# Feed-forward down projections by seven products of half blocks

## What is computed

```python
def rmsnorm(x, g):
    xf = x.astype(jnp.float32)
    xf = xf * lax.rsqrt(jnp.mean(xf * xf, axis=-1, keepdims=True) + EPS)
    return (xf * g.astype(jnp.float32)).astype(x.dtype)

def swiglu_ffn(x, w_up, w_down):
    gate, up = jnp.split(x @ w_up, 2, axis=-1)
    return (jax.nn.silu(gate) * up) @ w_down

# in both layers
h = h + swiglu_ffn(rmsnorm(h, norm_ffn[l]), ffn_w_up[l], ffn_w_down[l])
```

## Time and profile before

| what | before |
|---|---|
| median of 3 runs | 1588.88 us (1588.54 to 1588.92) |
| span of the profiled execution | 1588.5 us |
| instructions | 26988 |
| TensorE busy | 1557.8 us, 98% |
| VectorE busy | 1050.6 us, 66% |
| ScalarE busy | 816.2 us, 51% |
| GpSimd busy | 812.8 us, 51% |

### The profile page before, as it was taken

How to read it: one execution, slowest core, us unless ns; L and a number is a source line. 1 busy time by engine, 2 the same in 40 slices (tenths; PEclk the granted TensorE clock), 3 DMA queues, 4 the chain that set the end, 5 groups by cost and what they waited for, 6 DMA issues and landing times.

```text
span 1588.5 us, 26988 instructions
## 1 busy us (share of the span) xinstructions
PE 1557.8 (98%) x10227; PEld 1356.5 (85%) x10227; DVE 1050.6 (66%) x1622; ACT 816.2 (51%) x1334; POOL 812.8 (51%) x459
## 2 busy tenths in 40 slices
PE   6999999999999999999999999999999999999997
PEld 4888888888887878478998998988788998998996
DVE  6887587597597859977734643664666762572555
ACT  4555455355356535376633542654666652453453
POOL 1444345345345439827655654654116665564653
PEclk8999999999999999999999999999999999999999
DMA  9322322322323365712332332352112333233231
GB/s 376 140 93 80 120 83 91 119 82 90 119 81 102 128 116 153 187 53 81 107 119 80 106 119 81 105 182 96 54 41 68 106 112 100 93 106 115 85 117 69
DMA packets 53640, 172.86 MB, mean 109 GB/s; under 512 B 5403, under 2 KB 11580, under 8 KB 53052
## 3 DMA queue, kind: packets, MB, share of 16 engines
q1 hardware_dynamic: 47296, 159.90, 30.6%
q10 hardware_dynamic: 6268, 11.95, 3.2%
HBM read 165.48 MB, written 6.36 MB: 108 GB/s over the span
## 4 chain that ended last, share of the span: by engine, by line
PE 79%; DVE 3%; issue 2%; ACT 2%; POOL 2%; DVEq 0%; ACTq 0%; POOLq 0%
PE gps L2026 13%; PE gps L2028 12%; PE gps L2027 12%; PE gps L2449 6%; PE gps L2451 6%; PE gps L2450 6%; PE aps L2449 3%; PE aps L2451 3%; PE aps L2450 3%; PE gps L2386 2%; PE gps L2084 1%; PE gps L2086 1%; PE gps L2085 1%; POOL w_lo L619 1%; PE aps L2527 1%
## 5 line engine op out<-in xcount | busy, mean ns | idle before, releaser
L619 POOL TENSOR_TENSOR w_lo<-w_raw,w_hi 128x1024 fp32r<-128x1024 f32 x172 | 437.4, 2547 | 545.9 <-ACT w_hi L741 545.8
L2026 PE MATMUL gps<-xa_hi,w_hi 128*128 128x512 f32 x767 | 306.6, 400 | 2.6 <-DVE xa_lo L1380 2.6
L2027 PE MATMUL gps<-xa_lo,w_hi 128*128 128x512 f32 x767 | 299.9, 391 | 0.0
L2028 PE MATMUL gps<-xa_hi,w_lo 128*128 128x512 f32 x767 | 299.8, 391 | 0.0
L741 ACT CAST w_hi<-w_raw 128x1024 fp32r<-128x1024 f32 x172 | 180.0, 1046 | 155.6 <-PE gps L2028 75.2
L2026 PEld LDWEIGHTS gps<-xa_hi,w_hi 128*128 128x128 f32 x767 | 144.6, 188 | 35.3 <-DVE xa_lo L1380 4.1
L2028 PEld LDWEIGHTS gps<-xa_hi,w_lo 128*128 128x128 f32 x767 | 144.6, 188 | 31.1
L2027 PEld LDWEIGHTS gps<-xa_lo,w_hi 128*128 128x128 f32 x767 | 144.8, 189 | 27.6
L2026 PE MATMUL gps<-xb_hi,w_hi 128*128 128x512 f32 x378 | 148.2, 392 | 0.0
L2028 PE MATMUL gps<-xb_hi,w_lo 128*128 128x512 f32 x378 | 147.2, 389 | 0.0
L2027 PE MATMUL gps<-xb_lo,w_hi 128*128 128x512 f32 x378 | 147.1, 389 | 0.0
(11 more groups left out here) (428 smaller groups left out, 4324.9 us busy)
## 6 DMA issues: line engine op xcount, KB each, us to landing
w_raw<-weights_dram SPq DMA_DIRECT2D x268, 512.0 KB, 3.5
ada_w<-ada_in_dram SPq DMA_DIRECT2D x8, 1024.0 KB, 18.1
gates<-ret_tab_dram ACTq DMA_DIRECT2D x4, 1024.0 KB, 6.0
spread<-glu_scratch_dram SPq DMA_DIRECT2D x12, 270.0 KB, 5.1
rel_scratch_dram<-rel_rows ACTq DMA_DIRECT2D x1, 3072.0 KB, 34.5
x<-x_turned_dram SPq DMA_DIRECT2D x2, 1024.0 KB, 7.2
res<-xT_dram ACTq DMA_DIRECT2D x1, 2048.0 KB, 9.5
bias<-rel_scratch_dram ACTq DMA_DIRECT2D x1, 2048.0 KB, 9.8
```

Of the source, the lines that this page charges most:

```text
L619: TT(w_lo[:, j, :], w_raw[:, j, :], w_hi[:, j, :].bitcast(F32), ALU.subtract).then_inc(lo_ready[j], 1)
L2026: mm(gps[:, j, :], w_hi[:, j, w], x[0][:, k, :], start=k == 0, stop=False)
L2027: mm(gps[:, j, :], w_hi[:, j, w], x[1][:, k, :], start=False, stop=False)
L2028: last = mm(gps[:, j, :], w_lo[:, j, w], x[0][:, k, :], start=False, stop=k == blocks - 1)
```

## The change

Per layer, the down projections of the first two parts are made in the same way as the up projections. A part's 8 hidden chunks by 8 output chunks become four further pairs: two output chunks each, with the hidden rows as 2 x 2 blocks (chunks in two sets, even and odd, tokens in two halves). The third part's down projection stays `dense`. The list `FF_ORDER` gives the order of the now 30 pairs of a layer: eight ups of part 0, the first up of part 1, four downs of part 0, the other seven ups of part 1, the first up of part 2, four downs of part 1, the other five ups of part 2.

- TensorE (`seven_products`, formerly `up_pair`): waits before the first down pair of a part for all of its mixes and lows. The six pairs around the downs are written out instead of looped.
- VectorE: in parts 0 and 1 the multiply of the up row by `rstd` is left out; it comes after the down products, in `down_added`, which adds the result into `res`. The hidden mixes are made row by row as rows come (`hidden_low`), from the rows in PSUM and a copy of the even row in `hbuf`. `hidden_mix_low` subtracts all four mixes' high parts in one operation of 1024 elements, after each odd row.
- ScalarE: copies each even row to `hbuf` (`row_copy`), casts its first half, casts odd rows as before, and casts the four mixes in one operation of 1024 elements (`hidden_mix_high`). After the last down pair it casts the row that waited in `hbuf` (`early_high`); VectorE follows with `early_low`.
- Weights: the down matrices' tiles come in pair order; their number is the same.

The diff's core:

```diff
+MIXED_PARTS = 2
+def ff_order():
+    order, starts = [], [sum(FF_PARTS[:part]) for part in range(len(FF_PARTS))]
+    for part, n in enumerate(FF_PARTS):
+        order += [("up", part, k) for k in range(1 if part else 0, n)]
+        if part < MIXED_PARTS:
+            order += [("up", part + 1, 0)] + [("down", part, m) for m in range(KC // 2)]
+    return order, starts
...
+        hid_rows = hbuf[:, 0:4:2, :].rearrange("p a (b t) -> p a b t", b=2)
...
             def ffn(layer, hidden, norm, n_next, gain=None, dst=None):      # ScalarE
+                def row_copy(s, part, k):
+                    mixes = mixes_before(layer, part) + k // 2
+                    if mixes > 0:
+                        act.wait_ge(hid_mix_low, mixes)
+                    nc.scalar.copy(halves(hbuf[:, 0, :]), UP_ROWS[s]).then_inc(row_copied, 1)
+                def hidden_high(s, part, k):
+                    act.wait_ge(row_ready, hidden_at(layer, part, k) + 1)
+                    if part > 0 and k == 0:
+                        row_copy(s, part, k)
+                    elif part >= MIXED_PARTS:
+                        nc.scalar.copy(halves(hidden[:, k, :]), UP_ROWS[s]).then_inc(hid_high, 1)
+                    elif k % 2 == 1:
+                        nc.scalar.copy(hid_double(k // 2)[:, :, 0, :], UP_ROWS[s]).then_inc(hid_high, 1)
+                    else:
+                        row_copy(s, part, k)
+                        act.wait_ge(row_copied, copies_at(layer, part, k) + 1)
+                        nc.scalar.copy(hid_single(k // 2)[:, 0, :], hbuf[:, 0, 0:TH]).then_inc(hid_high, 1)
+                def early_high(part):
+                    if part < MIXED_PARTS:
+                        ins = nc.scalar.copy(hid_single(0)[:, 0, :], hbuf[:, 0, 0:TH])
+                    else:
+                        ins = nc.scalar.copy(hidden[:, 0, :], hbuf[:, 0, :])
+                    ins.then_inc(hid_high, 1)
+                def hidden_mix_high(f, part, m):
+                    act.wait_ge(rows_free, f + 3)
+                    nc.scalar.copy(hid_mix(layer, m, 0), hid_rows).then_inc(hid_mix_high, 1)
+                for n in range(FF_PAIRS):
+                    kind, part, k = FF_ORDER[n - 1] if n else (None, None, None)
+                    first_row_high(I1, s1)
+                    if kind == "up":
+                        silu(up + (n - 1) // 2, 1 - s)
+                    if n > 1:
+                        first_copy(f, I, s)
...
+                    copied(f, 4, GATE_ROW[s][:, TH:], UP_ROW[s])
+                    last_sum_high(f + 1, s1)
+                    if kind == "down" and k == KC // 2 - 1:
+                        act.wait_ge(tile_done[2 * (1 - s) + 1], up + (n - 1) // 2 + 2)
+                        early_high(part + 1)
+                    if kind == "up" and part < MIXED_PARTS and k % 2 == 1:
+                        hidden_mix_high(f - 1, part, k // 2)
...
             def ffn(layer, hidden_hi, hidden_lo, norm, n_next, build=None):  # VectorE
+                    if part >= MIXED_PARTS:
+                        own.done(TT(UP_ROWS[s], UP_ROWS[s], halves(rstd[:]), ALU.mult))
+                def down_added(n, m):
+                    dve.wait_ge(tile_done[2 * s + 1], I + 2)
+                    summed = own.mark(TT(UP_ROWS[s], UP_ROWS[s], halves(hbuf[:, 2 * s + 1, :]), ALU.add))
+                    first = own.mark(TT(GATE_ROW[s], GATE_ROW[s], rstd[:], ALU.mult))
+                    own.wait(summed)
+                    second = own.mark(TT(UP_ROWS[s], UP_ROWS[s], halves(rstd[:]), ALU.mult))
+                    own.wait(first)
+                    TT(res[:, 2 * m, :], GATE_ROW[s], res[:, 2 * m, :], ALU.add).then_inc(evicted[s], 1)
+                    own.wait(second)
+                    TT(halves(res[:, 2 * m + 1, :]), UP_ROWS[s], halves(res[:, 2 * m + 1, :]), ALU.add).then_inc(rows_free, 1)
+                def hidden_low(s, part, k):
...
+                    elif k % 2 == 1:
+                        two = hid_double(k // 2)
+                        dve.wait_ge(hid_high, high_at(part, k))
+                        TT(two[:, :, 1, :], UP_ROWS[s], two[:, :, 0, :].bitcast(F32), ALU.subtract).then_inc(hid_low, 1)
+                        own.wait(made["t1"])
+                        third = own.mark(TT(odd[:, TH:], second, even[:, 0:TH], ALU.subtract))
+                        TT(even[:, TH:], second, even[:, TH:], ALU.subtract)
+                        own.wait(third)
+                        TT(odd[:, 0:TH], first, odd[:, TH:], ALU.subtract).then_inc(rows_free, 1)
+                    else:
+                        one = hid_single(k // 2)
+                        dve.wait_ge(hid_high, high_at(part, k))
+                        TT(one[:, 1, :], first, one[:, 0, :].bitcast(F32), ALU.subtract).then_inc(hid_low, 1)
+                        made["t1"] = own.mark(TT(even[:, 0:TH], second, even[:, 0:TH], ALU.subtract))
+                        own.wait(made["t1"])
+                        dve.sem_inc(rows_free, 1)
+                def hidden_mix_low(part, m):
+                    dve.wait_ge(hid_mix_high, mixes_before(layer, part) + m + 1)
+                    TT(hid_mix(layer, m, 1), hid_rows, hid_mix(layer, m, 0).bitcast(F32), ALU.subtract).then_inc(hid_mix_low, 1)
+                def early_low(part):
...
+                    TT(one[:, 1, :], even[:, 0:TH], one[:, 0, :].bitcast(F32), ALU.subtract).then_inc(hid_low, 1)
+                    dve.wait_ge(hid_low, mixed_at(layer, part, 0) + 1)
+                    made["t1"] = own.mark(TT(even[:, 0:TH], even[:, TH:], even[:, 0:TH], ALU.subtract))
+                for n in range(FF_PAIRS):
...
+                        last_sum_low(f + 1, 1 - s)
+                    if n + 2 < FF_PAIRS:
+                        two_sums(up + (n + 2) // 2, f + 2, s)
+                    if kind == "down" and k == KC // 2 - 1:
+                        early_low(part + 1)
+                    if kind == "up" and part < MIXED_PARTS and k % 2 == 1:
+                        hidden_mix_low(part, k // 2)
...
             def ffn(layer_n, norm, x_mix, hidden):                           # TensorE
+                    for n in range(lead_down // 2 * 2, last_down // 2 * 2 + 2):
+                        if n == lead_down:
+                            pe.wait_ge(hid_low, mixed_at(layer_n, part + 1, 0))
+                            pe.wait_ge(hid_mix_low, mixes_before(layer_n, part + 1))
+                        kind, _, _ = FF_ORDER[n]
+                        seven_products(f0 + n, up + n // 2, n % 2, own_x if kind == "down" else x)
```

More of the change, by code:

```diff
@@ L118, in phase_starts @@
             sizes += [("kv", 4), ("q", KC), ("w_o", KC)]
[L119 to L120 removed]
+        sizes += [(f"up{layer}", 2 * FF_PAIRS), (f"down{layer}", KC)]
     at, starts = 0, {}
@@ L592, in ffn @@
             def ffn(layer):
[L593 to L599, removed]
+                f0, up, down = layer * FF_PAIRS, START[f"up{layer}"], START[f"down{layer}"]
+                loads(up, up + 1)
+                for m in range(FF_PAIRS // 2):
+                    loads_behind_sums(up + 1 + m, f0 + 2 * m)
+                loads(down + 1, down + KC // SLOTS)
+            loads(START["pw2"] + 1, START["up0"])
             ffn(0)
-            loads(START["kv"], START["up10"])
+            loads(START["kv"], START["up1"])
             ffn(1)
@@ L712, in ffn @@
             def ffn(layer):
[L713 to L727, removed]
+                f0, up, down = layer * FF_PAIRS, START[f"up{layer}"], START[f"down{layer}"]
+                norm = RMS_FF1 if layer else RMS_FF0
+                add_squares(norm, 1, 5)
+                pair_low(up, f0, 0)
+                add_squares(norm, 5, KC - 1)
+                pair_low(up, f0 + 1, 1)
+                with pool.Fori(1, FF_PAIRS // 2) as i:
+                    for s in range(2):
+                        pair_low(i + up, i * 2 + (f0 + s), s)
+                lows(down, down + KC // SLOTS)
+            lows(START["pw2"] + 1, START["up0"])
             ffn(0)
-            lows(START["kv"], START["up10"])
+            lows(START["kv"], START["up1"])
             ffn(1)
@@ L1221, in ffn @@
+                kind, part, k = FF_ORDER[-1]
+                w_high(down, 2)
+                silu(I, s)
+                hidden_high(s, part, k)
                 if layer == 0:
@@ L1941, in _ @@
+                kind, part, k = FF_ORDER[-1]
+                gate_and_up(FF_PAIRS - 1, part, k)
+                hidden_low((FF_PAIRS - 1) % 2, part, k)
+                residual(f"down{layer}", n_next, build=build)
             ffn(0, xa_hi, xa_lo, RMS_FF0, RMS_ATTN, (X_KV, lambda c: vcol("norm_kv", c), xb_hi, xb_lo))
@@ new lines, in ffn @@
+                quads(at, FF_PAIRS // 2)
+                n = FF_PARTS[-1]
+                ready_k = lambda k: pe.wait_ge(rows_free, f0 + FF_ORDER.index(("up", MIXED_PARTS, k)) + 3)
+                pe.wait_ge(hid_low, mixed_at(layer_n, MIXED_PARTS, 0) + 1)
```

(5 more changed lines are left out.)

291 lines of the change are left out of this document (147 added, 144 removed).

## The result

The changed kernel takes 1612.45 us in the median of four runs (1611.25 to 1615.2), the kernel before 1588.71 (four runs, 1587.71 to 1588.92): a ratio of 1.0156, 95% interval 1.0142 to 1.0169. It is slower, by 23.7 us where 16.9 were forecast, and 1.45 us above the predicted range. The profiled execution has a span of 1610.5 us, 22.0 more than before.

The account below looks back on a forecast made before the run. TensorE, busy 98% of the span, bounds the kernel by its matmuls' spacing. Terms -12.9 + 15.5 + 10.3 + 3.2 + 0.8 = +16.9 gave 1605.8 us from 1588.88; whole range 1587 to 1611.

Parts of the forecast that it names:

- Matmuls: Four down parts become four pairs each, 40.32 us for 43.55, so -3.23 each and -12.9 us in all.
- Weights and mixed rows: Same count of weight loads, nothing taken; even rows' copy and cast delay each layer's second pair by 0.4, +0.8 us.
- The mixes: `hidden_mix_low` waits behind GpSimd and delays the gate multiply; TensorE waits 1.29 us, twelve times, 15.5 us.
- Rival B: VectorE goes first at the mixes; TensorE waits 12 x 0.36 and 4 x 1.66; 1587.8 us, no change; chance 0.18.
- C: The mixes are hidden and only the matmuls count: 1576.8 us; chance 0.08.
- The boundaries: A part's first down pair waits for `hid_mix_low` before its first product: 2.58 us, four times, 10.3 us.
- Rows held over: After the last down pair `early_high` and `early_low` delay the gate multiply: waits of 1.4 and 0.2, two layers, 3.2 us.
- The step that failed: A granted clock fall after TensorE's 2.6 us stalls was named but given no time, as no row showed one.
- a rival with 0.07: GpSimd keeps its turn through the next subtraction too, 1628 us; a clock fall would work the same way; chance 0.07.

Follow-up runs that it names:

- the last three profiles: Changed kernel with all new waits taken away: mixes on GpSimd 1577.19 us, the same again 1578.14 us, mixes on VectorE behind the gate multiply 1579.3 us.

## Why the prediction was wrong in size

The side, the mechanism, the places and the counts were right; the growth was 6.8 us larger than forecast in the medians and the range ended 1.45 us too low. Net, 25.0 stand against 16.9. The ledger gives the difference: the clock 4.3, the late second matmuls 1.8, layer 1's mix 1.3, and 0.8 from small excesses of the terms that were in the sum.

- *Matmuls, -12.9.* Right: -6.45 in layer 0, and the net of -10.7 leaves the same for layer 1. The spacing of the earlier trace rows was the right price for the new products. The Trainium skill's isolated gap ("TensorE: Matmul & The Clock Gate", section Back-to-back issue gap), which made it an estimated 19 us, does not agree with these runs: their gain is 12.9.
- *Weights and mixed rows.* Nothing and +0.8: no wait for weights in these stages, and +0.43 in each layer's second pair.
- *The mixes.* GpSimd came first by 0.23, and from 762.02 + 1.16 = 763.18 the mix took its 1.2, to 764.39. The stall is 1.32, forecast 1.29. The margin was the forecast 0.23 in all sixteen mixes, so the order had been worked out and not guessed, thin as it was. Rival B's bound is met where VectorE goes first (a gap of 0.51, so 0.39, for 0.36), and C's sum of 1576.8 where no wait is left: 1577.2 and 1578.1, with layer 1's 1.3 in it.
- *The boundaries, 4 x 2.58.* Measured 2.60.
- *Rows held over, 3.2.* Measured 3.5.
- *The restart.* Each gap costs some 0.09 more, because the second matmul behind it comes late: 1.8 in all, taken as 0. The earlier trace rows ended with the stall's first matmul, and I did not look at the next.
- *Layer 1's mix.* +1.3, from a place that I took as untouched. The lock that I had read in the earlier trace rows for the new operation works as well between old ones, and a shift of 0.28 us turned the order there.
- **The step that failed.** "A fall of the granted clock after the 2.6 us stalls would work the same way; both stages read 1.00 and no row shows such a stall in them." From this I put the clock at nothing and left it to a rival with 0.07. It cost 4.3 us in the profiled execution. That no row showed it was a reason for an unknown cost with two ends, nothing and the loss of a stretch at the lower level, and that end belonged in the range; with it the range would have held the result. As the range was only 1.45 short, the 1.8 of the late second matmuls would have done it too; but those were not thought of, while the fall of the clock was named and then set to nothing.

The start of the program, up to 5.5 us apart between profiles, was in neither sum. It works on both kernels (the start lay 3.0 us earlier in the profile of after than in that of before), and it is why 23.7 in the medians, 22.0 in the profiled spans and 25.0 net all describe the same change.

## What to carry to other kernels

Before an operation with two SBUF inputs is put on VectorE, look at what GpSimd starts just ahead of it: here a GpSimd start 0.23 us ahead made 1.2 us of work 2.14, sixteen times over. Price a stall of the engine that sets the end at more than its length: gaps of 2.2 to 2.7 us were followed by a fall of the clock in 9 of 12 cases, and that was had back by splitting the wait across products or even by idle matmuls. And where a kernel's start varies, compare from a fixed matmul to the end.

## What the runs showed of the hardware

The granted clock against the length of TensorE's gap, from start to start, at the four boundaries of each profile: gaps of 1.26 and 1.27, no fall in 8; of 1.82, none in 8; of 2.18, a fall in 2 of 4; of 2.72, in 7 of 8; of 2.71 filled with matmuls, none in 4; of 0.2 or none (the last three profiles), none in 12. Each fall cost 1.3 to 1.5 us, in matmuls of 256 columns that started 0.213 and not 0.120 us apart. That gaps of the same length do both shows that the length alone doesn't decide; what else does was not tried.

VectorE against GpSimd, for an operation of 1.21 us with two SBUF inputs: 1.21 alone, 2.14 with GpSimd's 512-element subtraction 0.23 us ahead, 1.55 with it 0.83 ahead, 1.21 with one input in PSUM and GpSimd 0.23 ahead.
